# A two-layer decoder step on one core: layers unrolled, projections cut into parts of half the tokens, and the norms laid between the parts

## The chip, the cores and the metric

The kernel runs on one core of a Trainium2 chip. TensorE (PE) multiplies; VectorE (DVE), ScalarE (ACT) and GpSimd (POOL) work on the elements; SyncE (SP) issues most of the transfers. The metric is the device time of one launch, in microseconds (us).

## The reference, cut to what matters

One inference step of two layers, for 512 prompt tokens and 8 sample tokens that share the weights (520 tokens of 1024 features), all in float32:

```python
def decoder_layer(x, mem_kv, past, lp, rel_bias):
    g = lp['norm_g']
    mix, st = mixer_block(rms_norm(x, g[0]), lp, rel_bias, past)
    x = x + rms_norm(mix, g[1])
    x = x + rms_norm(cross_attention(rms_norm(x, g[2]), mem_kv, lp['w_xq'], lp['w_xo']), g[3])
    x = x + rms_norm(swiglu(rms_norm(x, g[4]), lp['w_ffn_in'], lp['w_ffn_out']), g[5])
    return x, st
```

`rms_norm` divides each token by the root of its mean square and multiplies by a gain. `mixer_block` projects the input with `w_in` (queries, keys and values, gates of the attention heads, the inputs of two convolutions, and 3 x 1024 merge gates), runs sparse attention (for the sample tokens over a paged cache), a convolution of 3 taps and one of 31 taps with a LayerNorm behind it, maps each of the three branches to 1024 features, merges them by the sigmoid of the gates, and projects with `w_o`. Cross-attention has 4 heads and 256 memory tokens; the feed-forward part has 2816 hidden features.

## The kernel before, in words

Activations lie transposed in SBUF: 128 features by 520 tokens is a chunk, 8 chunks are one token row of 1024 features (KC = 8). A projection goes in **units** of 128 output features, 512 KB of weights each. Float32 is split in a high and a low part, and a product is three matmuls (low weights by high activations, high by low, high by high) for each chunk and each half of the tokens (HALF = 260), so a unit of 8 chunks is 48 matmuls, issued by `products` (L422). SP loads a unit into a ring of four raw slots (L372); ACT makes the high part (`split_hi`, L381), DVE the low part (`split_lo`, L386), one unit ahead of PE. The matmuls of a layer in these stages: mix 960 in 20 units and 48 more for the head gates (L720), mg (merge gates) 1152, out (the three branch projections, L1753) 384, wo 384, xkv (keys and values of the memory, 256 columns) 192, xq 192, xo 192, fi (feed-forward in) 2112, fo (feed-forward out) 1056: 6672.

The layers run in a hardware loop, and so do groups of four units. Each step of a layer is a block of its own, and a block begins when every engine has ended the one before: the norm in front of mix, mix, convolutions and gathering of new rows (the conv block, L738 to L891), prompt attention, decode (sample attention over the cache), mg, the LayerNorm, out, wo, one block for norms 1 and 2, xkv, xq, cross-attention, xo, one block for norms 3 and 4, fi, fo, norm 5. `norm_block` has ACT square the chunks (L485), PE sum them over the features with 80 small matmuls in the trace (L499), DVE form the mean (L522), POOL raise it to -1/2 (L512), DVE build a diagonal (L526), PE spread it over the partitions (L505), DVE multiply (`t`, L536), and then either ACT and DVE or POOL make the high and low parts (L489, L470) or DVE and POOL add to x (L473). `stage_block` (L1592) converts a source that isn't normed, all 8 chunks of it, before PE starts (L1601 on ACT, L1612 on DVE). Three times in a layer a phase ends: a barrier, and POOL clears each semaphore of it (L143 to L148). The program starts with loads, 40 matmul rows for key biases (L315, two passes each in the trace), transposes of x and of the memory (L329), flips for the bias table (L337) and, in each layer, a block that loads and transposes the small vectors (L614 to L655).

These lines hold the order of the norm's work and the wait at the head of a stage:

```python
                            for c in range(KC):
                                e.wait_ge(sq_ready, KC * k + c + 1)
...
                            e.wait_ge(rstd_ready, k + 1)
...
                        if source is not None:
                            e.wait_ge(op_lo, base + chunks)
                        pe(e)
```

Of the kernel before, what the change touches and what calls it, by code (L numbers as in the profile page):

```python
# [1 line left out]

# [12 lines left out]
F32 = mybir.dt.float32  # L15
F32R = mybir.dt.float32r
I32 = mybir.dt.int32
# [34 lines left out]

V_GAIN, V_MEM, V_CA, V_CB, V_CG, V_CS, V_B1, V_B2, V_CC, V_PE, V_END = 0, 48, 56, 62, 64, 66, 68, 70, 72, 134, 166
RMS_EPS, LN_EPS = 1e-6, 1e-5
SEL_FORCE = 1e6


U_MIX, U_MG, U_OUT, U_WO, U_XKV, U_XQ, U_XO, U_FI, U_FO, U_END = 0, 20, 44, 52, 60, 68, 72, 80, 124, 148
# [64 lines left out]

def build(nc, A, O):
# [9 lines left out]

    @contextmanager
    def phase_semaphores():

        first = len(sems)
        with ExitStack() as scope:
            owner.append(scope)  # L140
            yield
            owner.pop()
            with nc.Block() as block:  # L143
# [7 lines left out]
    def sb(scope, name, shape, dt=F32):  # L151
        return scope.enter_context(nc.sbuf_tensor(name, shape, dt))

    def await_reg(e, s, value):

        e.wait_ge(s, value)
        e.sem_inc(passed, 1)

    with stack:

        xT = sb(stack, "xT", [P, KC, TOK])
        act_hi = sb(stack, "act_hi", [P, KC, TOK], F32R)
        act_lo = sb(stack, "act_lo", [P, KC, TOK], F32R)
        w_raw = sb(stack, "w_raw", [P, RING, KC * P])
        w_hi = sb(stack, "w_hi", [P, 2, KC * P], F32R)
        w_lo = sb(stack, "w_lo", [P, 2, KC * P], F32R)
        ident = sb(stack, "ident", [P, P])
        ones = sb(stack, "ones", [P, P])
        ov = sb(stack, "ov", [P, 2, SELB + 1])
        rt = sb(stack, "rt", [SELB + 1, 2 * P])  # L170
        key_bias = sb(stack, "key_bias", [P, 40, N_HEADS])
        new_bias = sb(stack, "new_bias", [NB, NB, N_HEADS])
        gather_rows = sb(stack, "gather_rows", [P, NB * 8], U32)
        vecs = sb(stack, "vecs", [P, V_END])
        minus_half = sb(stack, "minus_half", [P, NB])
        pg = stack.enter_context(nc.psum_tensor("pg", [P, 2, 2, 512], F32))
        pn = stack.enter_context(nc.psum_tensor("pn", [P, 2, 512], F32))
        pa = [stack.enter_context(nc.psum_tensor(f"pa{i}", [P, 512], F32)) for i in range(2)]
        line_dram = nc.dram_tensor("line_scratch", [N_HEADS, LINE], F32)
# [3 lines left out]
        passed = sem("passed")  # L183
        dve_chain, act_chain, pool_chain = Chain(sem("dve_done")), Chain(sem("act_done")), Chain(sem("pool_done"))
        raw_full = [sem(f"raw_full{i}") for i in range(RING)]
        whi_ready, w_ready = sem("whi_ready"), sem("w_ready")
        unit_done = sem("unit_done")
        evac = [sem("evac0"), sem("evac1")]
        sq_ready, sq_used, ms_ready, rstd_ready = (sem(n) for n in ("sq_ready", "sq_used", "ms_ready", "rstd_ready"))
        diag_ready, rstd_bc, t_ready, hi_ready, even_ended, odd_ended = (sem(n) for n in (  # L190
            "diag_ready", "rstd_bc", "t_ready", "hi_ready", "even_ended", "odd_ended"))
# [6 lines left out]


        with phase_semaphores(), ExitStack() as scope:  # L200
            x_nat = sb(scope, "x_nat", [P, 5, D_MODEL])
            m_nat = sb(scope, "m_nat", [P, 2, D_MODEL])
            m_sq = sb(scope, "m_sq", [P, D_MODEL])
            m_ms = sb(scope, "m_ms", [P, 2])
            m_rstd = sb(scope, "m_rstd", [P, 2])
            memT = sb(scope, "memT", [P, KC, N_MEM])
# [1930 lines left out]
```

## Time and profile before

| what | value |
|---|---|
| time, median of 3 runs (lowest, highest) | 4017.01 us (4013.03, 4021.43) |
| span of the profiled execution | 4001.0 us |
| TensorE busy | 3353.9 us, 84% of the span |
| VectorE, ScalarE, GpSimd busy | 1486.5, 958.4, 348.6 us |
| moved by transfers | 346.88 MB, mean 87 GB/s |

The span is the profiled execution from its first to its last instruction. The profile gives no other time for that execution; the median of the runs is 16.0 us over the span (4017.01 less 4001.0). Busy times are sums over an engine's instructions. A granted clock (PEclk) of 1.0 is 2.4 GHz, 0.5 is 1.2 GHz. A window view gives for a stretch, from a start to an end in us, the length, each engine's busy time with the count of its instructions, the mean granted clock, the busy share of the transfer engines and GB/s.

### The profile page before, as it was taken

How to read it: one execution, taken by the hardware profiler on the slowest of the kernel's cores; microseconds unless marked ns; L12 is line 12 of the kernel's file. 1: busy time of each engine (PE TensorE's matmuls, PEld its weight loads, DVE VectorE, ACT ScalarE, POOL GpSimd, SP SyncE). 2: the span in 40 equal slices, each digit the busy share in tenths (PEclk: the TensorE clock that was granted, in tenths of full speed). 3: DMA queues.
4: the chain of work that ended last, by engine and by line, in shares of the span. 5: the costliest groups of instructions: out<-in, count | busy, mean ns of one | idle time of the engine just before them, and what ended most of it. 6: DMA issues, size and time to landing. Idle time of an engine off the chain costs nothing. (4 is left out here: it accounts for less than half of the span.)

```text
span 4001.0 us, 61151 instructions
## 1 busy us (share of the span) xinstructions
PE 3353.9 (84%) x22906; PEld 3143.2 (79%) x22906; DVE 1486.5 (37%) x3364; ACT 958.4 (24%) x1827; POOL 348.6 (9%) x470
## 2 busy tenths in 40 slices
PE   3878799898988677899939788989979777879997
PEld 2876588887978577899939566888879676879997
DVE  1235533333553322333222454343436523133322
ACT  0223322211222212222212233121212222122221
POOL 1000032221000101000010002222200010010000
PEclk8887788887988676999959779888869878679998
DMA  4220154441322301232223104443313214013321
GB/s 127 64 97 17 56 178 151 137 137 63 95 66 66 140 18 32 80 93 86 67 41 89 72 14 151 148 159 128 132 46 91 58 38 152 17 47 89 94 87 45
DMA packets 353360, 346.88 MB, mean 87 GB/s; under 512 B 36001, under 2 KB 323110, under 8 KB 336238
## 3 DMA queue, kind: packets, MB, share of 16 engines
q1 hardware_dynamic: 334238, 210.34, 17.9%
q0 software_dynamic: 18944, 134.24, 9.7%
q8 instruction: 103, 1.69, 0.2%
q14 instruction: 75, 0.61, 0.1%
HBM read 333.85 MB, written 19.55 MB: 88 GB/s over the span
## 5 line engine op out<-in xcount | busy, mean ns | idle before, releaser
L422 PE MATMUL pg<-act_hi,w_lo 128*128 128x260 f32 x3328 | 682.4, 287 | 115.0 <-PEq L143 42.0
L422 PE MATMUL pg<-act_lo,w_hi 128*128 128x260 f32 x3328 | 679.3, 286 | 0.0
L422 PE MATMUL pg<-act_hi,w_hi 128*128 128x260 f32 x3328 | 679.1, 286 | 0.0
L386 DVE TENSOR_TENSOR w_lo<-w_raw,w_hi 128x1024 fp32r<-128x1024 f32 x296 | 362.5, 1225 | 690.7 <-ACT w_hi L381 682.8
L422 PEld LDWEIGHTS pg<-act_hi,w_lo 128*128 128x128 f32 x3328 | 523.8, 192 | 119.9 <-issue 89.3
L422 PEld LDWEIGHTS pg<-act_hi,w_hi 128*128 128x128 f32 x3328 | 522.3, 192 | 0.0
L422 PEld LDWEIGHTS pg<-act_lo,w_hi 128*128 128x128 f32 x3328 | 522.3, 192 | 0.0
L381 ACT CAST w_hi<-w_raw 128x1024 fp32r<-128x1024 f32 x292 | 305.7, 1047 | 291.3 <-PE pg L422 137.0
L499 PE MATMUL pa<-ones,sq 128*128 128x1 f32 (+1 forms) x960 | 173.4, 305 | 52.9 <-ACT sq L485 52.9
L499 PEld LDWEIGHTS pa<-ones,sq 128*128 128x128 f32 (+1 forms) x960 | 168.6, 263 | 61.1 <-ACT sq L485 57.4
L1418 ACT COPY w_raw<-pg 128x512 f32<-128x512 f32 x144 | 84.4, 586 | 443.1 <-PE pn L1315 421.2
L1391 PE MATMUL pn<-pr,v_sel 128*128 128x8 f32 x1024 | 185.5, 325 | 0.0
L1391 PEld LDWEIGHTS pn<-pr,v_sel 128*128 128x128 f32 x1024 | 184.4, 285 | 0.0
L1291 PE MATMUL pg<-ident,apart 128*128 128x128 f32 x1024 | 161.6, 309 | 14.1 <-DVE apart L1467 14.1
L512 POOL TENSOR_TENSOR r<-ms,minus_half 128x8 f32<-128x8 f32 x12 | 19.7, 1642 | 1647.2 <-DVE ms L523 1647.2
L1291 PEld LDWEIGHTS pg<-ident,apart 128*128 128x128 f32 x1024 | 133.8, 163 | 18.4 <-issue 15.1
L422 PE MATMUL pg<-hid_hi,w_lo 128*128 128x260 f32 x704 | 142.1, 283 | 6.1 <-PEq L1592 6.1
L422 PE MATMUL pg<-hid_hi,w_hi 128*128 128x260 f32 x704 | 141.5, 282 | 0.0
L422 PE MATMUL pg<-hid_lo,w_hi 128*128 128x260 f32 x704 | 141.3, 282 | 0.0
L1315 PEld LDWEIGHTS pn<-q_blk,w_raw 128*128 128x128 f32 x1024 | 134.5, 192 | 6.7
L1244 POOL COPY cell<-gather_rows 128x1 uint32 (+1 forms) x128 | 28.7, 224 | 1268.5 <-POOLq L143 703.7
L1246 POOL DMA_INDIRECT cache<-in_cache_kv,cell x128 | 129.1, 1009 | 70.4 <-POOL cell L1244 70.4
(395 smaller groups left out, 5107.3 us busy)
## 6 DMA issues: line engine op xcount, KB each, us to landing
w_raw<-in_w_ffn_in SPq DMA_DIRECT2D x88, 512.0 KB, 3.8
w_raw<-in_w_in SPq DMA_DIRECT2D x80, 512.0 KB, 3.8
cmem<-in_cache_mem SPq DMA_DIRECT2D x16, 1024.0 KB, 12.9
w_raw<-in_w_ffn_out SPq DMA_DIRECT2D x32, 512.0 KB, 3.7
win<-in_cache_win SPq DMA_DIRECT2D x16, 512.0 KB, 3.6
w_raw<-in_w_o SPq DMA_DIRECT2D x16, 512.0 KB, 3.8
w_raw<-in_w_xkv SPq DMA_DIRECT2D x16, 512.0 KB, 3.8
out_win_sample<-in_cache_win SPq DMA_DIRECT2D x2, 4088.0 KB
```

Source lines behind the costliest of these rows:

```text
L381: e.copy(w_hi[:, slot % 2, :], w_raw[:, slot, :]).then_inc(whi_ready, 1)
L386: e.tensor_tensor(w_lo[:, slot % 2, :], w_raw[:, slot, :], w_hi[:, slot % 2, :].bitcast(F32), ALU.subtract).then_inc(w_ready, 1)
L422: mm = e.matmul(pg[:, tslot, h, 0:wd], w[:, slot % 2, wk], x[:, k0 + k, at:at + wd], start=first and k == 0 and n == 0, stop=last and k == ...
L499: mm = e.matmul(pa[i][0:w, tt:tt + 1], sq[:, c % 2, tt * P:tt * P + w], ones[:, 0:1], start=c == 0 and tt == 0, stop=c == KC - 1, skip_gro ...
L512: e.tensor_tensor(r[:], ms[:], minus_half[:], ALU.pow).then_inc(rstd_ready, 1)
L1244: e.tensor_copy(cell[:, k % 4:k % 4 + 1], gather_rows[:, bass.ds(b * TILES + k, 1)]).then_inc(cell_set, 1)
L1246: e.indirect_dma_start(out=cache[:, k % 4, :], out_offset=None, in_=rows_dram, in_offset=bass.IndirectOffsetOnAxis(ap=cell[:, k % 4:k % 4 ...
L1291: mm = e.transpose(pg[:, 0, kv, at:at + P], apart[:, k % 2, 2 * kv + g, 2 * pair:2 * pair + 2, :].rearrange("p t d -> p (t d)"), ident[:])
L1315: mm = e.matmul(pn[:, 0, (4 * k + t) * 8:(4 * k + t + 1) * 8], k_sel[:, t * P:(t + 1) * P], q_of(b), start=True, stop=True)
L1391: e.matmul(pn[:, 1, 8:16], v_sel[:, par, t, :], pr[:, t, :], start=t == 0, stop=False)
L1418: e.copy(k_sel[:], pg[:, 1, 0, :]).then_inc(ks_ready, 1)
```

## The change

The two layers are written out in Python, so no loop is left around the projections. A stage is a list of `Part`s (unit, tile, half of the tokens, a range of chunks), and the lists decide the order of PE's matmuls: `head` does half 0 of four tiles first, in two runs of four chunks, then half 1; `both` does one tile's halves in turn; `tail` ends with all of half 0 before all of half 1. Each (tile, half) has one of four banks of PSUM. Raw weights have three slots, split weights four, and splits run two units ahead.

The norms are no blocks now. An `Edge` joins one stage to the next: when a part is done ACT squares it and copies it (`post_evict`), POOL adds the squares (`post_sum`), PE sums them over the features in three matmuls (`stats`), POOL raises to -1/2 (`power`), PE spreads (`spread`), DVE multiplies (`t_step`), DVE for even and POOL for odd chunks adds to x (`x_step`), ACT makes the high part and the squares for the next norm (`hi_step`), DVE the low part (`lo_step`), POOL adds the squares (`acc_step`). The 1/rms of the norm ahead of a product isn't applied to the activations any more; DVE multiplies the product by it when it empties PSUM (`scaled_evict`). PE waits per chunk (`gate`), not for a whole conversion. Of the other steps: setup work lies between the units of the first mix, the head gates are tile 20 of mix, the LayerNorm's pieces lie between mg's last tiles, the 31-tap convolution is done in 4 taps per mg unit instead of 3, the memory's conversion lies under wo, the memory cache is loaded at the start of cross-attention (it was ahead of it, L1812), sums of the merge are on POOL, and the key biases are made in layer 0's conv block from two loads into one buffer, the second of which waits for the matmuls of the first. Semaphores are cleared after setup, and in each layer after decode and after cross-attention. The bodies of prompt attention, decode and cross-attention are as they were.

The core of the diff:
```diff
-            def norm_block(norms):
...
-                            for c in range(KC):
-                                e.wait_ge(sq_ready, KC * k + c + 1)
-                                for tt in range(5):
-                                    w = P if tt < 4 else NB
-                                    mm = e.matmul(pa[i][0:w, tt:tt + 1], sq[:, c % 2, tt * P:tt * P + w], ones[:, 0:1],
-                                                  start=c == 0 and tt == 0, stop=c == KC - 1, skip_group_check=True)
...
-                        if source is not None:
-                            e.wait_ge(op_lo, base + chunks)
-                        pe(e)
...
+def head(tiles, cuts0=((0, 4), (4, 4)), cuts1=((0, 4), (4, 4))):
+
+    return [Part(t, t, h, k, kn, k, k == 0, k + kn == KC) for h, cuts in enumerate((cuts0, cuts1)) for k, kn in cuts for t in tiles]
+def both(tiles):
+    return [Part(t, t, h, 0, KC, 0, True, True) for t in tiles for h in range(2)]
+def tail(tiles):
+    return [Part(t, t, h, 0, KC, 0, True, True) for h in range(2) for t in tiles]
...
+        mix = lambda: Stage(self, 21, head(range(4)) + both(range(4, 21)))
...
+            self.wo.append(Stage(self, 8, head(range(4), ((0, 7), (7, 1)), ((0, KC),)) + tail(range(4, 8))))
+            self.xkv.append(Stage(self, 8, [Part(t, t, 0, 0, KC, 0, True, True) for t in range(8)]))
+            self.xq.append(Stage(self, 4, head(range(4))))
+            self.xo.append(Stage(self, 4, [Part(t // 2, t, h, XH * (t % 2), XH, 0, True, True) for h in range(2) for t in range(KC)]))
+            self.fi.append(Stage(self, 44, head(range(4)) + both(range(4, 44))))
...
+                for k in range(x.kn):
+                    if gate is not None:
+                        signal, count = gate(x.half, x.xk + k)
+                        e.wait_ge(signal, count)
...
+        def post_evict(e, ed, i, t, h):
+            st, n = ed.before, 2 * KC * ed.post + i
+            tile_done(e, st, t, h, handed=True)
...
+            e.activation(ed.sqa[:, i % 3, :], bank_of(st, t, h), ACT.Square).then_inc(sqa_ready, 1)
+            e.copy(ed.Y[:, h, t, :], bank_of(st, t, h)).then_inc(emptied(st, t, h), 1)
+        def post_sum(e, ed, i, t, h):
...
+                e.tensor_tensor(ed.acc1[:, h, :], ed.acc1[:, h, :], ed.sqa[:, i % 3, :], ALU.add).then_inc(acc1_ready, 1)
+        def stats(e, ed, i):
...
+            for s, a in enumerate((0, P, HALF - P)):
+                mm = e.matmul(pa[0][:, 3 * i + s:3 * i + s + 1], acc[:, h, a:a + P], ones[:, 0:1], start=True, stop=True)
...
+        def hi_step(e, ed, h, c):
...
+            e.activation(act_hi[:, h, c, :], x, ACT.Copy, scale=col(ed.gain_pre + c)).then_inc(hi_ready, 1)
...
+            e.activation(ed.sqb[:, (KC * h + c) % 3, :], x, ACT.Square).then_inc(sqb_ready, 1)
+        def scaled_evict(e, ed, st, t, h, dst, handed=False):
+            tile_done(e, st, t, h, handed)
+            e.wait_ge(rbc_ready, 2 * ed.pre + h + 1)
+            e.tensor_tensor(dst, bank_of(st, t, h), rbc[:, h, :], ALU.mult).then_inc(emptied(st, t, h), 1)
...
+                        if L == 0:
+                            for i in range(2):
+                                if i:
+                                    e.wait_ge(keys_mm, 1)
+                                e.dma_start(keys[:], C["keys"].ap()[:, i * 20 * P:(i + 1) * 20 * P]).then_inc(keys_in, 16)
+                        e.wait_ge(nt_used, 11)
...
+                    run(e, wo, act, 0, 17, w_gate)
+                    stats(e, ed, 0)
+                    run(e, wo, act, 17, 18)
+                    spread(e, ed, 0)
+                    run(e, wo, act, 18, 20)
+                    run(e, skv, mem_act, 0, 1, m_gate, N_MEM)
+                    stats(e, ed, 1)
```

PE's program at its start. Names: `x_nat` is x as loaded, `keys` and `rel` make the key biases, `sq` are squares of a norm, `act_hi` and `w_lo` a high and a low part. Before:

```order
L313 MATMUL pn<-line1h,rel 8x512 x2
L315 MATMUL pg<-rel,keys 128x8 x40
L329 MATMUL pa<-ident,x_nat 128x128 x32
L329 MATMUL pa<-ident,x_nat 128x8 x8
L329 MATMUL pa<-ident,m_nat 128x128 x16
L337 MATMUL pg<-toep_up,flip 128x512 x8
...
L650 MATMUL pa<-ident,rows_pe 128x32
...
L505 MATMUL pn<-diag,ones 128x260 x2
L476 UNCONDITIONAL_BRANCH
L712 UNCONDITIONAL_BRANCH
L422 MATMUL pg<-act_hi,w_lo 128x260 x2
```

And now:

```order
L989 MATMUL pn<-ident,rows_g 128x112
L997 MATMUL pa<-ident,x_nat 128x128 x16
L997 MATMUL pa<-ident,x_nat 128x8 x4
...
L1001 MATMUL pn<-ident,rows_m 128x96
L1002 MATMUL pn<-ident,rows_c 128x124
L563 MATMUL pg<-act_hi,w_lo 128x260
```

The first product stands behind the transposes of x and of small vectors alone; the key biases (now L1193, 40 rows in layer 0's conv block), the memory and the bias table come later, and there are no sums of squares ahead of it.

PE's program between wo and xkv in layer 0. `mem_hi` is the high part of the memory, `acc_wo` the sum of squares, `r_t` the 1/rms per token. Before:

```order
L422 MATMUL pg<-act_hi,w_hi 128x260 x2
...
L1592 UNCONDITIONAL_BRANCH
L491 UNCONDITIONAL_BRANCH
L499 MATMUL pa<-ones,sq 128x1 x4
L499 MATMUL pa<-ones,sq 8x1
...
L505 MATMUL pn<-diag,ones 128x260 x2
...
L422 MATMUL pg<-mem_hi,w_lo 128x256
```

And now, around the third `stats` and `spread`, which lie inside xkv:

```order
L563 MATMUL pg<-mem_hi,w_hi 128x256
...
L636 MATMUL pa<-ident,r_t 128x128 x2
L636 MATMUL pa<-ident,r_t 128x4
L563 MATMUL pg<-mem_hi,w_lo 128x256
```

Two norms of 40 small rows each stood between the last product of wo and the first of xkv; now three rows of `stats` and two of `spread` stand between products, four times from wo's tail to xq.

POOL's program at the norms between xo and fi. `t_xo` is the scaled product, `sqa_xo` and `sqb_xo` squares for the norm behind xo and the one ahead of fi. Before:

```order
L512 TENSOR_TENSOR r<-ms,minus_half 128x8
L473 TENSOR_TENSOR xT<-xT,t 128x520 x4
...
L470 TENSOR_TENSOR act_lo<-t,act_hi 128x520 x4
...
L148 ISA x17
```

And now, from the norm's first power to the second:

```order
L607 TENSOR_TENSOR acc_xo<-acc_xo,sqa_xo 128x260 x2
L628 TENSOR_TENSOR r_t<-ms_t,minus_half 128x3
...
L656 TENSOR_TENSOR xT<-xT,t_xo 128x260
L607 TENSOR_TENSOR acc_xo<-acc_xo,sqa_xo 128x260
L675 COPY acc_xo<-sqb_xo 128x260
...
L678 TENSOR_TENSOR acc_xo<-acc_xo,sqb_xo 128x260
```

POOL had 10 instructions of a norm pair here and clears of semaphores behind them; it now has 44 of half the width (16 sums behind xo, 16 ahead of fi, 8 additions to x, 4 powers), and PE's `stats` waits for its sums.

## Rows read from the trace of the kernel before

**Rows 1.** Page, busy time of each engine and its instructions; granted clock in 40 slices.

```profile
span 4001.0 us, 61151 instructions
...
PE 3353.9 (84%) x22906; PEld 3143.2 (79%) x22906; DVE 1486.5 (37%) x3364; ACT 958.4 (24%) x1827; POOL 348.6 (9%) x470
...
PEclk8887788887988676999959779888869878679998
```

**Rows 2.** Windows, layer 0: start:end length, busy by engine, clock, DMA share, GB/s.

```profile
0.00:134.90 134.90, 55.60 (x242) 44.82 (x242) 29.53 (x56) 15.55 (x23) 17.79 (x28) 0.73 0.37 96
134.90:264.90 130.00, 125.73 (x1009) 125.35 (x1009) 25.94 (x22) 31.64 (x42) 0.00 (x0) 0.96 0.27 73
264.90:293.50 28.60, 10.86 (x77) 8.83 (x77) 17.56 (x45) 9.44 (x24) 0.00 (x0) 0.67 0.56 215
1008.40:1013.60 5.20, 0.05 (x1) 0.08 (x1) 0.00 (x0) 0.00 (x0) 0.00 (x0) 0.50 0.00 2
1013.60:1179.30 165.70, 147.10 (x1184) 145.30 (x1184) 98.87 (x168) 46.10 (x61) 1.68 (x1) 0.93 0.33 89
1179.30:1237.30 58.00, 47.78 (x384) 47.57 (x384) 42.18 (x65) 12.62 (x16) 0.00 (x0) 0.91 0.25 73
1237.30:1285.10 47.80, 47.75 (x384) 47.62 (x384) 9.18 (x8) 10.78 (x14) 0.00 (x0) 0.97 0.27 77
1285.10:1353.10 68.00, 33.94 (x169) 31.27 (x169) 24.64 (x50) 19.16 (x34) 15.14 (x10) 0.52 0.07 23
1353.10:1410.70 57.60, 51.20 (x384) 50.30 (x384) 14.43 (x12) 15.28 (x22) 0.00 (x0) 0.91 0.65 229
1411.60:1521.00 109.40, 90.06 (x471) 85.41 (x471) 25.67 (x41) 14.89 (x45) 0.00 (x0) 0.65 0.03 10
1525.80:1867.20 341.40, 315.08 (x2472) 311.48 (x2472) 127.16 (x149) 95.43 (x126) 15.12 (x10) 0.91 0.26 76
...
1611.00:1867.20 256.20, 256.18 (x2112) 255.97 (x2112) 98.55 (x108) 68.71 (x87) 0.00 (x0) 0.99 0.31 90
1870.20:1997.20 127.00, 126.96 (x1056) 126.75 (x1056) 28.18 (x23) 27.04 (x30) 0.00 (x0) 1.00 0.26 76
1997.20:2097.10 99.90, 33.72 (x172) 30.68 (x172) 21.09 (x37) 17.55 (x27) 15.41 (x11) 0.52 0.19 35
3953.00:4001.00 48.00, 23.56 (x125) 19.79 (x124) 16.42 (x27) 5.57 (x9) 8.31 (x5) 0.61 0.11 45
```

**Rows 3.** Groups by line on DVE and ACT: count, busy us, mean ns, idle before.

```profile
L386 DVE TENSOR_TENSOR w_lo<-w_raw,w_hi 128x1024 fp32r<-128x1024 f32 x296 | 362.5, 1225 | 690.7 <-ACT w_hi L381 682.8
...
L1669 DVE SCALAR_TENSOR_TENSOR y_c<-u_c,vecs,y_c 128x512 f32<-128x512 f32 x120 | 90.0, 750 | 2.8
...
L1669 DVE SCALAR_TENSOR_TENSOR y_c<-us_c,vecs,y_c 128x8 f32<-128x8 f32 x120 | 27.2, 227 | 4.2
...
L2030 DVE SCALAR_TENSOR_TENSOR silu<-thf,pg 128x520 f32<-128x520 f32 x44 | 30.6, 696 | 115.8 <-ACT thf L2021 115.8
...
L381 ACT CAST w_hi<-w_raw 128x1024 fp32r<-128x1024 f32 x292 | 305.7, 1047 | 291.3 <-PE pg L422 137.0
```

**Rows 4.** Groups by line on POOL, and the key-bias matmuls on PE.

```profile
L473 POOL TENSOR_TENSOR xT<-xT,t 128x520 f32<-128x520 f32 x24 | 40.1, 1672 | 43.8 <-DVE t L536 43.8
...
L470 POOL TENSOR_TENSOR act_lo<-t,act_hi 128x520 fp32r<-128x520 f32 x24 | 30.8, 1284 | 59.5 <-ACT act_hi L489 59.5
...
L512 POOL TENSOR_TENSOR r<-ms,minus_half 128x8 f32<-128x8 f32 x12 | 19.7, 1642 | 1647.2 <-DVE ms L523 1647.2
...
L315 PE MATMUL pg<-rel,keys 32*128 32x8 f32 x80 | 17.2, 356 | 0.0
```

**Rows 5.** Timeline, SP's queue: start, us, line, transfer.

```profile
274.10 11.48 SPq L754 DMA_DIRECT2D out_kv_sample<-nat  x1
...
1376.08 8.04 SPq L1812 DMA_DIRECT2D cmem<-in_cache_mem  x8
```

**Rows 6.** Timeline, PE at the start of fi.

```profile
1611.53 0.64 PE L422 MATMUL pg<-act_lo,w_hi 128*128 128x260 f32 x2
```

More of the change, by code:

```diff
@@ L121, in restart, with __init__, take @@
         self.n = 0
+class Strip:
+    def __init__(self, nc, start, end):
+        self.nc, self.at, self.end = nc, -(-start // 32) * 32, end
+    def take(self, name, shape, dt=F32):
+        size = -(-4 * int(np.prod(shape[1:])) // 32) * 32
+        start, self.at = self.at, self.at + size
+        assert self.at <= self.end, (name, self.at, self.end)
+        return self.nc.alloc_sbuf_tensor_at(name, shape, dt, offset=start)
+@dataclass
+class Part:
+    unit: int
+    tile: int
+    half: int
+    wk: int
+    kn: int
+    xk: int
+    first: bool
+    last: bool
+    to: str = "pg"
+    end: int = 0
+    bank: int = 0
+    turn: int = 0
@@ L124, in build, with order, step @@
+@dataclass
+class Edge:
+    post: int
+    pre: int
+    seq: int
+    before: Stage
+    gain_post: int
+    gain_pre: int
+    Y: object = None
+    acc1: object = None
+    acc2: object = None
+    sqa: object = None
+    sqb: object = None
+    t: object = None
+    free: tuple = (0, 0)
+    @property
+    def order(self):
+        return [(x.tile, x.half) for x in self.before.parts if x.last]
+    def step(self, i):
+        return self.seq + (i if self.post >= 0 else i - 2) + 1
 def build(nc, A, O):
@@ new lines, in _, with flips @@
+                    run(e, mix0, act, at(10), at(15))
+                    def flips(i):
+                        e.wait_ge(toep_in, 16 * (i + 1))
+                        e.wait_ge(line_ready, 1)
+                        for n in range(i * HPG, (i + 1) * HPG):
+                            if n >= 2:
+                                e.wait_ge(flip_used, n - 1)
+                            e.matmul(pn[:, n % 2, :], flip[:], toep_up[:, n % HPG, :], start=True, stop=True).then_inc(flip_done, 1)
+                    flips(0)
@@ new lines, in build @@
+        for_dec.at = ends_at
+        for_dec.end = ends_at + 2048 + 384
+        second = for_dec.take("second", [P, 2, 2 * P + 1])
+        for_dec = Strip(nc, late_at, z_at)
+        gate_dg = for_dec.take("gate_dg", [NG_W, NB, NG_W])
+        gate_bc = for_dec.take("gate_bc", [P, NB, NG_W])
+        for_dec = Strip(nc, decode_at, limit)
+        xkv0 = for_dec.take("xkv0", [P, 2, 512])
+        xkv = (xkv0, xkv1)
+        k_sel = for_dec.take("k_sel", [P, 512])
+        cv = for_dec.take("cvs", [P, 2, P])
@@ L790, in _ @@
                         mm.then_inc(pem, 1)
+                        if L == 0:
+                            for i in range(2):
+                                e.wait_ge(keys_in, 16 * (i + 1))
+                                for b in range(20):
+                                    at = (20 * i + b) * N_HEADS
+                                    mm = e.matmul(pg[:, 1, 1, at:at + N_HEADS], keys[:, b * P:(b + 1) * P], rel[:], start=True, stop=True)
+                                mm.then_inc(keys_mm, 1)
                         e.wait_ge(ua_ready, 1)
@@ L2079, in build @@
+        rows_out = Strip(nc, mid_at, limit).take("rows_out", [P, 5, D_MODEL])
+        with phase_semaphores("end"):
             y_tr, y_cp, y_out = sem("y_tr"), sem("y_cp"), sem("y_out")
```

2448 lines of the change are left out of this document (1483 added, 965 removed).

## The prediction

> **What bounds the kernel now.** I read the page first, then windows by stage, then groups by line. PE is busy 3353.9 us of 4001.0, far above every other engine [rows 1], so the question is where PE stands still and where it runs at the lower clock. The row of the clock gives both places: full in some slices, half in others. The windows sort them. In fi 2112 matmuls fill 256.2 us without a hole, in fo 1056 fill 127.0 us [rows 2]: 127.0/1056 = 120.3 ns a matmul, so a unit of 48 takes 5.77 us. This part can't get faster unless the number of matmuls falls, and it doesn't. DVE and ACT need 1.225 and 1.047 us a unit to split the weights [rows 3]; SP's transfers use about a third of the time.
>
> The other kind of window is the norm. Between wo and xkv 68.0 us pass, with PE busy 33.94 at clock 0.52; between the end of fo and the next mix 99.9 us, PE busy 33.72 at 0.52; before the first product of all 134.9 us [rows 2]. PE's busy time there is mostly small matmuls at half speed, and one engine after another has the word. So each stage has its own limit: projections are PE's, seams are a chain over five engines.
>
> **The change, part by part.** Times are of the profiled execution (span 4001.0); its sum is made against the span, and 16.0 us are added at the end, since the median of the runs stands so much higher.
>
> *Start of layer 0.* From 0 to the conv block it takes 134.9 + 130.0 = 264.9 us [rows 2]. Now x is the first large load. 2.1 MB at the 229 GB/s seen around xq is 9 us, say 10 with the issue; about half (an estimate) of PE's 21 us of transposes and flips is x's (55.60 less 17.2 for the keys [rows 4] and about 17 for a norm, half of 33.94), so transposes end near 18.5, and the first product begins about 22.5 after one high and one low part. Four head tiles need 23.1 us and wait some 5 for chunks: 51. Seventeen units more are 98.1, the other half of the transposes and flips, laid between them, 11, and 3 for its waits: 163; 5 for the last eviction and the block. The conv block starts at 168: **-97**. Ends: -75 if weights and x share the queue so that the first product comes at 45; -110 if nothing waits.
>
> *Keys in the conv block.* The trace shows this block's queue stuck: one small output transfer cost SP 11.48 us of issuing, until 285.58 [rows 5], because the copy of the sample window, issued earlier in the block, fills the queues. SP is free of it 20.7 us into the block; I take 24 until a load issued behind the copy has landed, and the first half of the keys is such a load. On the path now: 24 + 8.6 (half of 17.2 [rows 4]) + 2.5 for the second load (an estimate; it waits for PE, and the outputs wait behind it on SP) + 8.6 + 5 for the ends, then the 3 us lead of prompt attention: 51.8 against 28.6 [rows 2]: **+23**. Ends: +8 if the load gets through half-way in the copy; +30 if the second load is as slow as the copy. DVE's 17.56 us in this block lie under it.
>
> *Each layer.* One clearing of semaphores less ahead of decode, a longer one behind it (5.20 us with PE idle now [rows 2]) and the first split behind that: +2.6. mg and LayerNorm, 165.7 us: 1152 matmuls are 138.6; 2 for the clock's climb; about 6 for LayerNorm's own sums and spreading between tiles; and DVE has 1.225 + 0.70 (eviction, as L2030) + 4 x (0.750 + 0.227) = 5.83 us a unit [rows 3], about 6.1 with the gaps between dependent instructions, against PE's 5.77, over 16 units 5 us, of which banks hide some: 3. Together 149.6, **-16**. Out, 58.0: the conversion that stood ahead of wo goes, 384 x 0.1203 = 46.2, **-12**. Wo, 47.8: 49.2 with the first chunks' wait, +1.4. From wo's end to xq's end 68.0 + 57.6 = 125.6: two norms run under xkv's 192 matmuls; 46.2 remain for xkv and xq, and I allow 9.5 for five small-matmul stops and for xq's first chunk, 55.7, **-70**. Cross to xo +2: the memory cache now is loaded at cross's start. Its issue took 8.04 us [rows 5], the window in which it was moved had 229 GB/s, so its 8.4 MB take 37 us at most at that rate, shared then with weights; transfers are idle in cross-attention (share 0.03 of 109.4 us [rows 2]), and the sample part, which needs it, comes behind the prompt part, some 40 us in (an estimate: over a third of the stage). Hidden, with little to spare; without that cover 37 us a layer. Xo to fi's end, 341.4: 2304 matmuls are 277.2, 3 for two climbs, and 16 for the head of fi (power 1.642 on POOL [rows 4], spreading, then t, x, high, low for the first chunk, and splits that stand behind xo's units): 296, **-45**. Fo -1.5. A layer: 2.6 - 16 - 12 + 1.4 - 70 + 2 - 45 - 1.5 = -138.5; two layers **-277**.
>
> *Between the layers.* From fo's end to the first product 99.9 us [rows 2], and 24.7 for the first four units. Now 23.1 + 8 for the chain until the first low part + 7.5 for the second half's chunks, small stops and the climb = 38.6, **-86**. Ends of the seam terms: nothing below, if the chains overlap in full; above, half of now's 68.0 for each, as a rival below. The rest of mix (130.0 for 1008 matmuls in layer 0, 8.7 over 121.3) loses another -6.
>
> *End.* 48.0 us from fo's end [rows 2]: half 0 of the last norm runs under the last tile's half 1, the chain of half 1 and the transposes stay, 25: **-23**.
>
> Sum: -97 + 23 - 277 - 92 - 23 = -466. Each place where PE stops long enough to come back at 1.2 GHz costs about 2 us: at fi's start two matmuls end in 0.64 us [rows 6], and 256.2 is 2.1 over 2112 x 0.1203. I allow seven more of these, 14. 4001.0 - 466 + 14 = 3549, and 16 on top: **3565 us**.
>
> *The unknown price is POOL's.* An edge with two norms has 16 + 16 sums, 8 additions and 4 powers. The trace has no 128x260 sum on POOL. From below half of 1.284 us, 0.64; from above the whole 1.672 [rows 4]. I take 0.84, half of the nearest row, an addition of two SBUF operands. Then an edge is 40 x 0.84 + 4 x 1.642 = 40 us of POOL, spread over two tails and a head of about 60 us. At 0.64 the waits shrink; at 1.67 it is 73 us and POOL sets the seam.
> The rows show POOL's addition (1.672) slower than its subtraction of the same size (1.284); beside the first DVE runs its own addition of x and t, beside the second mostly a product that reads PSUM. The Trainium skill, "SBUF — State Buffer", section "Who interferes with whom", says why this may be and speaks against the change: a DVE instruction with two SBUF inputs and a GpSimd instruction that reads SBUF shut each other out for a whole instruction. By that rule a sum that meets a weight split waits up to 1.225 us more, 0.64 + 1.225 = 1.87, and an edge's 12 sums and additions between the first spread and the next stage's first statistics could take 12 us longer. The 0.39 us in the rows agree in sign, and nothing in this trace shows it against a split.
>
> **Rivals.**
> *Seams stay, shorter (POOL).* For: `stats` waits for POOL's last sum, and POOL's program is in a fixed order, so an addition to x stands behind sums. Against: POOL is busy 9% now. With 1.67 instead of 0.84, 12 instructions between spread and statistics cost 10 us a half; one half of it shown at five seams, and splits late behind it, with half clock in each: 50 to 130 us. **About 3650**.
> *Nearly no stalls.* The allowances above (9.5, 16, 3 and 6 a layer, 14 for the clock, 8 between layers, 23 for keys) halve: -65. **About 3500**.
> *The change doesn't do what it says.* Post-norms of the last tile can't overlap; if each seam also waits for the whole other half (splits, banks still full), five seams give back 34 us each, half of 68.0: **about 3735**.
> *Slower than before.* PE's program is straight, without loops. If PE were fed more slowly, each of 13,344 projection matmuls would lengthen. The 452 us forecast are gone at 34 ns each, a spacing of 154 ns instead of 120. Place: fi and fo, where nothing else can wait. For: idle time put down to PE's own sequencer at block starts. Against: the loops' bodies already hold 192 matmuls, and the spacing in them is that of the engine, not of its feed. **About 4060** at 157 ns. The Trainium skill, "Runtime: NRT & Kernel Launch", section "Instruction fetch mechanics", has instructions prefetched in sequence and only taken branches stall; no run here shows straight code of this length.
>
> **How the numbers follow.** Forecast 0.50, with a range of its own of 3525 to 3610: keys (-15, +7), start (-13, +22), conv-tap and head allowances. POOL seams 0.24, stall-free 0.13, not as described 0.08, slower 0.04; 0.01 for no change. Slower and unchanged are 0.05 together. The range of 8 in 10 takes in the forecast, stall-free from 3490, and POOL seams to 3680. A change of 0.2% is about what can be told from none here.
>
> **What would show it.** Right: the first matmul of L563 near 22 us and the conv block near 168; key biases some 24 us into that block; 120 ns in fi and fo; no stretch with clock near 0.5 but attention; holes of under 8 us between wo and xq and ahead of fi; mg near 150. Wrong: POOL sums of 1.5 us or more with PE waiting for them; PE waiting for splits in mg by more than 0.5 us a unit; cross-attention waiting for the memory cache; PE spacing above 125 ns; holes of 20 us at seams.

## The result, and the profile after

The changed kernel takes 3592.40 us (median of 4 runs, 3591.09 to 3594.55), against 4015.02 for the kernel before (4 runs, three of them those of the table under "Time and profile before"): a ratio of 0.8967, 95% interval 0.8943 to 0.8990. The forecast was 3565, with 3490 to 3680 for 8 in 10. The profiled execution has a span of 3590.3 us and took 3592.02.

The page of the changed kernel, the lines that answer to [rows 1]:

```profile
span 3590.3 us, 57484 instructions
...
PE 3210.2 (89%) x22207; PEld 3012.9 (84%) x22207; DVE 1573.9 (44%) x3626; ACT 950.6 (26%) x2036; POOL 524.5 (15%) x706
...
PEclk9957898887799966999999678888879999599999
```

TensorE has 144 us less to do, nearly all of it small matmuls of norms that ran at half clock; its idle time fell from 647 us (4001.0 less 3353.9) to 380. VectorE and GpSimd do more than before. The sums of squares on TensorE, in the page of the kernel before:

```profile
L499 PE MATMUL pa<-ones,sq 128*128 128x1 f32 (+1 forms) x960 | 173.4, 305 | 52.9 <-ACT sq L485 52.9
```

In the changed kernel they are 144 matmuls (L619) of 19.0 us together.

Windows of the changed kernel, columns as in [rows 2]. In layer 0: first product to conv block, conv block, mg, out, wo, xkv with xq, fo; then the conv block of layer 1 and the end. Below them, two longer stretches, fo's start to the end of the next mix, and fo's start in layer 1 to the end of the program; then xo with fi, fo's end to the end of mix, and cross-attention in layers 0 and 1.

```profile
25.10:172.70 147.60, 137.46 (x1066) 131.10 (x1067) 57.39 (x84) 31.61 (x50) 13.11 (x15) 0.97 0.46 124
172.70:226.70 54.00, 34.79 (x156) 31.38 (x156) 18.17 (x47) 9.99 (x24) 0.00 (x0) 0.50 0.34 130
946.70:1093.80 147.10, 146.92 (x1196) 146.48 (x1197) 111.28 (x184) 44.48 (x59) 2.27 (x1) 0.98 0.34 90
1093.80:1152.00 58.20, 49.22 (x386) 47.95 (x385) 27.43 (x44) 11.04 (x14) 20.46 (x14) 0.97 0.26 73
1152.00:1206.40 54.40, 50.08 (x400) 49.29 (x399) 20.17 (x28) 24.96 (x54) 15.97 (x21) 0.97 0.35 107
1206.40:1264.40 58.00, 51.63 (x420) 50.66 (x419) 34.25 (x57) 23.18 (x50) 24.54 (x27) 0.97 0.33 92
...
1686.70:1814.60 127.90, 127.90 (x1068) 127.72 (x1066) 32.28 (x34) 33.45 (x57) 12.15 (x17) 1.00 0.36 95
...
1956.30:1984.90 28.60, 16.76 (x76) 13.64 (x76) 17.56 (x45) 9.79 (x24) 0.00 (x0) 0.51 0.56 218
3565.60:3590.30 24.70, 9.50 (x52) 7.15 (x52) 16.12 (x31) 0.65 (x2) 6.83 (x9) 0.69 0.23 87
...
1686.50:1954.10 267.60, 260.60 (x2114) 258.95 (x2112) 86.69 (x116) 65.66 (x111) 35.87 (x45) 0.97 0.34 88
3437.50:3590.30 152.80, 137.59 (x1122) 135.04 (x1120) 45.95 (x63) 31.05 (x56) 18.94 (x26) 0.95 0.25 77
1386.80:1686.70 299.90, 290.02 (x2354) 288.71 (x2355) 155.98 (x235) 99.96 (x185) 35.86 (x44) 0.97 0.30 87
1814.60:1954.10 139.50, 132.50 (x1045) 131.04 (x1044) 54.41 (x83) 32.20 (x54) 23.72 (x29) 0.94 0.31 81
...
1264.40:1386.80 122.40, 97.05 (x472) 92.10 (x472) 28.37 (x47) 17.67 (x51) 0.00 (x0) 0.61 0.20 78
3021.90:3137.50 115.60, 89.98 (x472) 85.34 (x472) 28.41 (x47) 17.70 (x51) 0.00 (x0) 0.65 0.21 82
```

The seams are where the time came from: wo's end to xq's end is 58.0 us (125.6 before), xo's start to fi's end 299.9 (341.4), fo's end to the end of the next mix 139.5, the end 24.7 (48.0) [rows 2]. Two windows stand out on the other side. Out takes 58.2 us for 384 matmuls, no better than before with the wait ahead of wo in it, and layer 0's conv block 54.0 where layer 1's takes 28.6.

What TensorE waited for in all, in the view of waits (total us, times, longest):

```profile
PE pg L563 <- DVE w_lo L540: 31.5, 10, 8.7
...
PE pn L563 <- DVE G L2108: 16.4, 12, 1.9
...
PE pg L1193 <- DMA keys<-c_keys: 13.4, 2, 9.3
...
PE pn L636 <- POOL r_t L628: 7.4, 5, 2.5
```

The longest entry, for low parts of weights, lies for 16.7 us at mg's start behind decode (8.7 and 8.0 in the two layers); the others are waits of up to 3.1 us where a stage starts. The waits for GpSimd's powers (L628) are small. The one for `G` (L2108) comes twelve times, up to 1.9 us each, and TensorE's product into `pn` that waits stands in out alone.

### The profile page after: what moved, and what is told of

Its sections match the earlier page's. It is cut to its first block and busy times, and to the rows that moved or that the text cites. A ratio compares the mean times of both kernels' runs of the same rounds, so it can differ in the third digit from the quotient of the medians.

```text
span 3590.3 us, 57484 instructions
## 1 busy us (share of the span) xinstructions
PE 3210.2 (89%) x22207; PEld 3012.9 (84%) x22207; DVE 1573.9 (44%) x3626; ACT 950.6 (26%) x2036; POOL 524.5 (15%) x706
## 5 line engine op out<-in xcount | busy, mean ns | idle before, releaser
L563 PE MATMUL pg<-act_hi,w_lo 128*128 128x260 f32 x3360 | 972.0, 289 | 72.5 <-DVE w_lo L540 31.5
L563 PE MATMUL pg<-act_hi,w_hi 128*128 128x260 f32 x3360 | 962.9, 287 | 0.0
L563 PE MATMUL pg<-act_lo,w_hi 128*128 128x260 f32 x3360 | 961.1, 286 | 0.0
L563 PEld LDWEIGHTS pg<-act_lo,w_hi 128*128 128x128 f32 x3360 | 647.1, 193 | 0.5 <-issue 0.5
L563 PEld LDWEIGHTS pg<-act_hi,w_hi 128*128 128x128 f32 x3360 | 646.9, 193 | 0.0
L540 DVE TENSOR_TENSOR w_lo<-w_raw,w_hi 128x1024 fp32r<-128x1024 f32 (+1 forms) x290 | 354.3, 1226 | 475.4 <-ACT w_hi L534 473.1
L534 ACT CAST w_hi<-w_raw 128x1024 fp32r<-128x1024 f32 (+1 forms) x290 | 296.8, 1033 | 298.2 <-PE pg L563 118.2
L1665 PE MATMUL pg<-xkv,w 128*128 128x256 f32 x1024 | 262.4, 402 | 0.5
L1665 PEld LDWEIGHTS pg<-xkv,w 128*128 128x128 f32 x1024 | 198.7, 205 | 27.2 <-ACT second L1763 0.7
L1673 PEld LDWEIGHTS pn<-q_blk,k_sel 128*128 128x128 f32 x1024 | 134.5, 192 | 6.7
```

The lines of the kernel that those rows point to most:

```text
L534: e.copy(w_hi[:, v % RING, 0:n], w_raw[:, v % RAW, 0:n]).then_inc(whi_ready, 1)
L540: e.tensor_tensor(w_lo[:, v % RING, 0:n], w_raw[:, v % RAW, 0:n], w_hi[:, v % RING, 0:n].bitcast(F32), ALU.subtract).then_inc(w_ready, 1)
L563: mm = e.matmul(out, w[:, v % RING, wk], a[x.half][:, x.xk + k, :], start=x.first and k == 0 and n == 0, stop=x.last and k == x.kn - 1 and ...
L1665: e.matmul(pg[:, 1, 1, kv * 256:(kv + 1) * 256], w1[:, kv, 2 * (k % 4) + pair, :], xkv[k % 2][:, kv, pair * 256:(pair + 1) * 256], start=k ...
L1673: mm = e.matmul(pn[:, 0, (4 * k + t) * 8:(4 * k + t + 1) * 8], k_sel[:, t * P:(t + 1) * P], q_of(b), start=True, stop=True)
```

## The experiments

Times scatter by as much as most of the effects sought (below), so each experiment is judged by the windows of the stage that it changes; its whole time is given beside that.

**A circle in out.** The timeline of the changed kernel in out, one tile of the merge, all engines (TensorE's other products left out):

```profile
1109.54 1.70 POOL L1958 TENSOR_TENSOR G<-G 128x520 f32<-128x520 f32 x1 [4.83 <-DVE G L2108]
...
1111.31 1.30 POOL L1960 TENSOR_TENSOR G<-G 128x520 f32<-128x520 f32 x1
1112.64 0.64 ACT L2017 ACTIVATE act_hi<-G 128x520 fp32r<-128x520 f32 x1 [6.33 <-POOL G L1960]
1113.19 1.04 ACT L534 CAST w_hi<-w_raw 128x1024 fp32r<-128x1024 f32 x1
1114.26 1.23 DVE L540 TENSOR_TENSOR w_lo<-w_raw,w_hi 128x1024 fp32r<-128x1024 f32 x1 [4.19 <-ACT w_hi L534]
1115.40 0.69 DVE L2105 SCALAR_TENSOR_TENSOR G<-G,pg 128x520 f32<-128x520 f32 x1
...
1117.42 0.39 PE L563 MATMUL pn<-src_hi,w_lo 128*128 128x260 f32 x1 [1.88 <-DVE G L2108]
1117.44 1.69 POOL L1958 TENSOR_TENSOR G<-G 128x520 f32<-128x520 f32 x1 [4.83 <-DVE G L2108]
```

From one merge sum to the next 7.90 us pass (1117.44 less 1109.54), and no engine is busy all that time. ScalarE's program has the high part of a tile, which waits for GpSimd's sums, ahead of the split of the weights that VectorE must split before it can merge the next tile. So each tile's merge waits for the sums of the last. The first edit opens the circle by order alone:

```diff
+                    def high_of(m):
+                        e.wait_ge(sum_odd, 2 * (KC * L + m + 1))
+                        e.activation(act_hi[:, :, m, :], halves(G[:, m, :]), ACT.Copy, scale=0.5).then_inc(mrg_hi, 1)
                     for m in range(KC):
                         ahead_hi(e, out.u0 + m, wo.u0 + 2)
-                        e.wait_ge(sum_odd, 2 * (KC * L + m + 1))
-                        e.activation(act_hi[:, :, m, :], halves(G[:, m, :]), ACT.Copy, scale=0.5).then_inc(mrg_hi, 1)
+                        if m:
+                            high_of(m - 1)
+                    high_of(KC - 1)
```

> In the out stage ScalarE makes the high part of a merged tile one tile later, behind the weight split that it stood ahead of; nothing else changes. Theory: the stage runs in a circle over engines, merge on VectorE 2.0 us, two sums on GpSimd 3.0, high part 0.64, ScalarE's split 1.04, VectorE's split 1.23, which is the 7.9 us a tile that the trace shows, against 5.77 of products; with the high part behind the split the circle is open, out falls from 58.2 us to 47 to 49 in each layer, and the time by 18 to 22 us, to about 3572. Rival: GpSimd's sums are slow because VectorE holds the SBUF port, and the merge waits for them anyway; then out stays over 55 us and the time falls by less than 6 us.

Window of out in layer 0:

```profile
1100.90:1147.20 46.30, 46.30 (x388) 46.30 (x387) 35.23 (x45) 12.01 (x15) 26.30 (x14) 1.00 0.33 92
```

58.2 us became 46.3 in layer 0 and 46.2 in layer 1, with TensorE busy throughout; 3574.60 us (3563.91 to 3578.83). GpSimd needs longer for its sums now (26.30 us busy against 20.46): the second sum of a tile and the next weight split on VectorE meet, and six times in this window the sum takes 2.17 us for 1.30 and the split 2.33 for 1.23. That costs nothing here. The rival is out. The second way to shorten the circle undoes a part of the change, with ScalarE's order left:

```diff
                 @block.gpsimd
...
-                        e.tensor_tensor(g[0], g[0], g[1], ALU.add).then_inc(sum_odd, 1)
...
                 @block.vector
...
                         mm.then_inc(merged, 1)
+                        e.wait_ge(merged, KC * L + m + 1)
+                        e.tensor_tensor(g[0], g[0], g[1], ALU.add).then_inc(sum_odd, 1)
```

The second sum moves with the first.

> The two sums of the merge in out go back from GpSimd to VectorE (0.70 us each, as before the change); order on ScalarE as in the changed kernel. Theory of the circle: 2.0 + 1.4 + 0.64 + 1.04 + 1.23 = 6.3 us a tile, so out takes about 51 us in each layer, 13 to 15 us less in all, about 3578. Rival (the sums aren't in any circle, VectorE is what out lacks): VectorE gets 11 us more work a layer, and out stays at 58 us or grows.

```profile
1088.10:1136.70 48.60, 47.64 (x387) 46.55 (x386) 37.29 (x59) 12.63 (x16) 0.00 (x0) 1.00 0.31 88
```

48.6 us in each layer, somewhat better than the 51 worked out; 3574.18 us (3562.26 to 3578.91). VectorE has 10 us more work and the stage is still 9.6 shorter. Both agree: what out lacked was no engine; it was held by the length of the chain through three of them, VectorE, GpSimd and ScalarE.

**Keys in layer 0's conv block.** The first edit moves only the copy that the prediction held responsible:

```diff
-                        e.dma_start(o_layer("win_sample")[:, :, 0:WINDOW - 1].rearrange("o b w k g d -> (o b) w (k g d)"),
-                                    A["cache_win"][L:L + 1][:, :, 1:WINDOW].rearrange("o b w k g d -> (o b) w (k g d)")).then_inc(outs, 16)
...
+                        e.dma_start(O["win_sample"][L:L + 1][:, :, 0:WINDOW - 1].rearrange("o b w k g d -> (o b) w (k g d)"),
+                                    A["cache_win"][L:L + 1][:, :, 1:WINDOW].rearrange("o b w k g d -> (o b) w (k g d)")).then_inc(win_out, 16)
                         e.wait_ge(mn_cp, 4)
```

> The 4 MB copy of the sample window is issued behind the loads of the memory cache in cross-attention, not at the start of the conv block, in both layers. Theory: the copy is what the key-bias loads wait for; layer 0's conv block falls from 54.0 us to about 36, layer 1's from 28.6 to about 25, and nothing comes back in cross-attention, whose transfers are idle: 18 to 24 us less, about 3571. Rival: the two dependent loads and the 80 small matmuls set the block by themselves, or cross-attention waits for the memory cache beside the copy: the block stays over 48 us or cross grows by 10, and the time falls by less than 6 us.

PE's timeline in the conv block of the changed kernel, the two runs of key-bias matmuls:

```profile
198.57 8.70 PE L1193 MATMUL pg<-rel,keys 32*128 32x8 f32 x40 [9.33 <-DMA keys<-c_keys]
211.34 8.70 PE L1193 MATMUL pg<-rel,keys 32*128 32x8 f32 x40 [4.08 <-DMA keys<-c_keys]
```

The same view with the copy moved:

```profile
188.63 8.70 PE L1191 MATMUL pg<-rel,keys 32*128 32x8 f32 x40
201.26 8.70 PE L1191 MATMUL pg<-rel,keys 32*128 32x8 f32 x40 [3.94 <-DMA keys<-c_keys]
```

And windows of both conv blocks and of cross-attention in layer 0:

```profile
172.20:216.50 44.30, 34.69 (x156) 31.33 (x156) 18.19 (x47) 9.97 (x24) 0.00 (x0) 0.50 0.20 64
1944.50:1972.70 28.20, 16.82 (x77) 13.67 (x77) 17.55 (x45) 9.77 (x24) 0.00 (x0) 0.51 0.23 77
1252.80:1375.20 122.40, 96.94 (x473) 92.08 (x472) 28.44 (x47) 17.74 (x51) 0.00 (x0) 0.61 0.28 112
```

The wait of 9.33 us ahead of the first half is gone, so the copy did hold it; cross-attention is as long as without it, 122.4. But the block falls by 9.7 only, to 44.3: neither the theory's 36 nor the rival's 48. A block of 36 us would have needed the keys' matmuls some 8 us into it (25.9, where they began, less 18); at half clock TensorE's other small matmuls take until 16.4 (188.63 less 172.20). Layer 1's block hardly changes (28.2 us, for the 25 expected). The time is 3581.45 us (3575.47 to 3586.81). The next edit removes both waits: all keys are loaded in setup, on three groups of partitions:

```diff
-        keys = for_conv.take("keys", [NBUCK, 20 * P])
+        keys = Strip(nc, decode_at, limit).take("keys", [3 * NBUCK, 14 * P])
...
-                                    mm = e.matmul(pg[:, 1, 1, at:at + N_HEADS], keys[:, b * P:(b + 1) * P], rel[:], start=True, stop=True)
+                                mm = e.matmul(pg[:, 1, 1, b * N_HEADS:(b + 1) * N_HEADS], keys_of(b), rel_of(b), start=True, stop=True)
```

> All keys of the bias are loaded during setup into free space (on three groups of partitions, with three copies of the bias table); their 40 matmul rows stay where they are in layer 0's conv block. Theory: the block's 54.0 us are 28.6 of before, 9.3 of wait for the first load (behind the window copy), 4.1 for the second, and the rest of 17.4 us of matmuls at half clock; without the two waits it is 40 to 41 us. Rival: the block is held by something else that takes the same time, its outputs behind the copy of the window on SP's queue; then it stays over 48 us.

Windows of the conv block and of all between the first product and it:

```profile
176.10:211.50 35.40, 29.67 (x157) 26.83 (x157) 18.17 (x47) 9.86 (x24) 0.00 (x0) 0.60 0.46 180
24.20:176.10 151.90, 138.16 (x1067) 131.80 (x1067) 57.34 (x84) 31.59 (x50) 13.07 (x15) 0.96 0.46 125
```

And the keys' row in PE's timeline, without a wait:

```profile
187.78 17.48 PE L1195 MATMUL pg<-rel,keys 32*128 32x8 f32 x80
```

The block is 35.4, better than 40 to 41: both waits are gone, and in this execution the clock rose inside the block (0.60 against 0.50). The early loads cost mix 4 us (151.9 against 147.6; TensorE's second wait for a weight split there is 6.10 us, 2.49 in the changed kernel). 3585.75 us (3577.57 to 3589.53). The third place for them is mix itself:

```diff
+                    for b in range(40):
...
+                        mm = e.matmul(pa[1][:, b * N_HEADS:(b + 1) * N_HEADS], keys_of(b), rel_of(b), start=True, stop=True)
...
                     run(e, mix0, act, at(17), at(19))
```

> The keys are loaded as in e5, and their matmul rows stand in layer 0's mix between tiles 16 and 17; also ScalarE's order in out as in e1. Theory: conv block 28 to 29 us in layer 0 as in layer 1 (25 less), mix longer by what 40 small rows take beside full-size products (9 to 18 us), out 46.2 in both layers (24 less): 33 to 40 us less than the changed kernel, 3552 to 3560. Rival: weights, splits or evictions stand still behind the small rows and mix loses 25 us or more, so that moving the keys gives nothing and the time is that of e1, about 3570.

```profile
192.90:220.80 27.90, 11.91 (x76) 9.54 (x76) 17.55 (x45) 9.86 (x24) 0.00 (x0) 0.62 0.56 218
24.40:192.90 168.50, 155.98 (x1147) 149.25 (x1147) 58.02 (x86) 31.53 (x50) 13.17 (x15) 0.92 0.42 112
```

The keys' matmuls in mix:

```profile
143.50 14.77 PE L1061 MATMUL pa<-rel,keys 32*128 32x8 f32 x80
```

The conv block gives 26.1 us back, mix takes 20.9 of them, more than the 9 to 18 expected: the keys' matmuls take 14.77 us beside full products, not much less than the 17.4 alone, the wait for the second weight split is 2.2 longer (4.72 against 2.49), and the other 4 weren't followed. In time it is 3560.43 us (3559.14 to 3567.65), most of it from out. The keys belong in the conv block, where TensorE has room, with their loads ahead.

**Waiting by chunk.**

```diff
-            return lambda h, c: (lo_ready, 2 * KC * ed.pre + KC * h + c + 1)
+            return lambda h, c: (lo_ready, 2 * KC * ed.pre + KC * h + 4 * (c // 4) + 4)
```

> Behind the norms, TensorE waits for chunks in fours instead of one by one (the first product of a head waits for low part 4 instead of 1). Theory: the gain at the seams comes from laying norms beside other parts, and waiting by chunk gives little, since the runs of four chunks over four tiles last 11.5 us and the next chunks come in less: 1 to 3 us at each of the four heads that wait, 4 to 10 us in all, 3597 to 3603. Rival: waiting by chunk is what hides the conversions; then each head of xq, fi and mix pays the three chunks that it now waits for, 4 us with a restart at half clock, at six heads and in both halves: 20 us or more.

Windows of xo with fi, and of fo's end to mix's end:

```profile
1385.50:1686.50 301.00, 286.99 (x2354) 286.51 (x2355) 155.89 (x235) 99.95 (x185) 35.86 (x44) 0.98 0.30 87
1814.40:1954.80 140.40, 128.80 (x1045) 128.44 (x1044) 54.41 (x83) 32.19 (x54) 23.71 (x29) 0.95 0.32 81
```

1.1 and 0.9 us longer than in the changed kernel (299.9 and 139.5). TensorE starts fi 5 us later, and its waits at fi's head are 4 us longer in all: 7.0, 0.4 and 4.9 us in place of five of 0.8 to 2.7. But its busy time in the stretch is 3.0 us less (286.99 against 290.02), at a mean clock of 0.98 against 0.97, which takes most of that back. The theory holds, at its lower end; the time (3603.36 us, 3598.43 to 3605.55) is longer by more than these stages explain, and the rest lies in stages that the edit doesn't touch: in the profiled execution layer 1's cross-attention alone is 7 us longer (122.6 against 115.6).

**GpSimd's part in the seams.**

```diff
-            if c % 2 == 0:
-                x_step(e, ed, h, c)
+            x_step(e, ed, h, c, True)
```

(and GpSimd's own calls do nothing)

> All additions to x are on VectorE (0.45 us each); GpSimd, which had the odd chunks (0.75 to 0.92 us each, in a fixed order between its sums), keeps the sums and powers. Theory: the heads of xq, fi and mix are held by VectorE's chain and by the weight splits in it, and by the climb of the clock; GpSimd isn't the limit, so from xo's start to fi's end stays within 3 us of 299.9, mix of layer 1 within 3 us of 139.5 with its lead. Rival: GpSimd's place in the chain (its order, and the port that it shares with VectorE) sets the seams; then each of these stretches falls by 5 us or more, and the time by 15 or more.

```profile
1385.90:1685.60 299.70, 289.15 (x2354) 287.60 (x2355) 161.57 (x243) 100.28 (x185) 29.11 (x36) 0.97 0.30 87
1813.60:1954.00 140.40, 131.89 (x1045) 130.37 (x1044) 58.06 (x90) 32.62 (x54) 16.39 (x21) 0.94 0.32 81
```

299.7 and 140.4: within 1 us, though GpSimd is relieved of 7 us in each. Its additions aren't the bound of the seams. Its sums and powers stayed where they were; in the changed kernel TensorE's waits for them add up to 14.6 us over both layers. 3589.60 us (3584.20 to 3606.19).

**One half beside the other.**

```diff
-            + [part(KC - 1, i, h) for h in range(2) for i in range(3)])
+            + [part(KC - 1, i, h) for i in range(3) for h in range(2)])
```

> Fo's last tile is computed with its two halves in turn, so the first half of the tokens ends 2 us before the second and not 8; TensorE's statistics of both halves stand behind the last product. Nothing else changes. Theory: a norm of one half hides beside the products of the other; without that the chain of the first half lies bare after fo, 5 to 7 us more between fo and mix in layer 0 and 4 to 7 more behind fo in layer 1: 9 to 14 in all. Rival: the seam is held by the second half's chain or by VectorE and the splits, whatever the first half does: both stretches stay within 2 us.

Windows of fo's start to mix's end, and of fo's start in layer 1 to the end (267.6 and 152.8 in the changed kernel):

```profile
1682.00:1953.10 271.10, 260.88 (x2114) 259.24 (x2112) 86.97 (x116) 65.60 (x111) 37.10 (x45) 0.96 0.33 87
3439.80:3596.90 157.10, 139.40 (x1121) 136.72 (x1120) 46.14 (x63) 31.06 (x56) 19.07 (x26) 0.93 0.25 75
```

3.5 and 4.3 us longer, 7.8 in all. Behind fo it is 4.8 and 5.6, 10.4 in all, as the theory has it (9 to 14); fo itself is 1.3 us shorter in each layer, without the statistics in its last tile. 3599.81 us (3597.93 to 3605.05). Laying one half's norm beside the other half's products is worth some 4 us net at a seam of this shape.

**Both repairs.** ScalarE's order of e1, and the keys of e5 with their loads later in setup:

> The order on ScalarE of e1 and the keys of e5, their loads later in setup (behind the weights of tile 14), so that mix doesn't wait for them. Theory: the two waits are independent and add: out 46 us in both layers (24 less), layer 0's conv block about 35 (18 less), mix of layer 0 as in the changed kernel: 40 to 44 us less than the changed kernel in these stages, 3548 to 3556 with the scatter of decode and cross-attention. Rival: what is gained in out is lost in wo, or the later loads still hold weights or the bias table up: less than 32 us.

```profile
170.90:211.30 40.40, 34.91 (x157) 31.49 (x157) 18.18 (x47) 10.01 (x24) 0.00 (x0) 0.50 0.41 158
1086.90:1133.20 46.30, 46.30 (x388) 46.30 (x387) 35.22 (x45) 12.01 (x15) 26.34 (x14) 1.00 0.32 92
```

Out gives 11.9 us (12.0 in layer 1), the conv block 13.6 (at clock 0.50, so not the 18 of e5), and mix of layer 0 is no longer than in the changed kernel (146.1 against 147.6): some 39 in these stages, just under the 40 to 44 expected. The time is 3558.18 us (3553.69 to 3561.32), 2 above the expected range and 34 under the changed kernel's median, and no run of one reaches those of the other; its ratio to the kernel before is 0.8874 (0.8862 to 0.8886).

## Why the prediction was right, and where it was off

The direction and the mechanism were right: projections kept their price (fo 127.9 us for 1056 matmuls, 121 ns each), and the seams gave the time. Of the 410.7 us between the two spans 143.7 are TensorE's busy time and 267.0 its idle time. Which part of the change gave how much at the seams is argued and not shown: the experiments on single parts (e3, e7, e9) move 0 to 6 us a seam, and no run takes the rest apart. Term by term, with what was measured:

- *Start*, 168: 172.7. *Keys*, 51.8 for the block: 54.0, made as described but for sizes: the first half came at 25.9 us for 24, the second load cost 4.1 for 2.5.
- *mg*, 149.6: 147.1. *Wo's end to xq's end*, 55.7: 58.0. *Xo to fi's end*, 296: 299.9. *Fo*, 125.5: 127.9. *Fo's end to the end of mix*, with the lead of the conv block, 138: 141.7 (1814.6 to 1956.3). *End*, 25: 24.7. *Cross-attention* waits nowhere for the memory cache, as forecast. These are within 5 us each, but for cross-attention, which came out at 122.4 and 115.6 for 117 (more on it in the last section).
- *Wo*, 49.2: 54.4. TensorE does 18 products and then waits 3.2 us for the seventh low part of the merge; some 16 products behind it start 0.22 us apart instead of 0.12, at half clock, and the statistics lie in wo's tail. Only a wait of 3.0 was in the sum. E1 takes 1.1 of it back.
- *Out* is the step that failed, as mis-sized work: "384 x 0.1203 = 46.2" took TensorE for the bound, with no term for the sums that had moved to GpSimd and the conversion that had moved into ScalarE's loop. They closed a circle of 7.9 us a tile. 12 us a layer, 24 in all; e1 and e4 show it.
- *16 us on top of the span* was wrong. Every execution with both on record takes 1.7 or 1.8 us over its span (3592.02 for 3590.3). By that the profiled execution of the kernel before took about 4003 us, a quick one among executions of 3992.46 to 4023.61. The sum for the span, 3549, was 41 us under the 3590.3 measured, and the 16 hid part of this: that 3565 came within 28 us is in part luck.
- *14 us for the clock* aren't to be seen as a term of their own; the terms that exceed their forecast by 2 to 5 us hold such restarts, as wo's does.
- *The stall-free rival*: the allowances that it halves add up to 114 us by its own list, so half is 57 and not 65, and its time about 3508. That changes no reading.
- One sign didn't come: the conv blocks of both layers, and not attention alone, ran at a clock near 0.5 (0.50 and 0.51).

The price of GpSimd's sum was taken well: 0.75 to 0.91 us in the mean (0.84 taken). Additions to x took longer, 0.85 to 1.07 by edge, and powers less, 0.91 for the 1.642 taken.

Groups by line on GpSimd in the changed kernel, its slowest and its quickest kind of sum:

```profile
L678 POOL TENSOR_TENSOR acc_wo<-acc_wo,sqb_wo 128x260 f32<-128x260 f32 x28 | 25.5, 912 | 2.6 <-ACT sqb_wo L668 0.3
...
L607 POOL TENSOR_TENSOR acc_fo<-acc_fo,sqa_fo 128x260 f32<-128x260 f32 x28 | 21.0, 751 | 187.6 <-ACT sqa_fo L597 187.6
```

And the timeline between xo and fi, two sums on GpSimd and a weight split on VectorE:

```profile
1407.31 0.74 POOL L607 TENSOR_TENSOR acc_xo<-acc_xo,sqa_xo 128x260 f32<-128x260 f32 x1
1408.55 1.50 POOL L607 TENSOR_TENSOR acc_xo<-acc_xo,sqa_xo 128x260 f32<-128x260 f32 x1 [0.50 <-ACT sqa_xo L597]
...
1408.22 1.23 DVE L540 TENSOR_TENSOR w_lo<-w_raw,w_hi 128x1024 fp32r<-128x1024 f32 x1 [2.24 <-ACT w_hi L534]
```

A sum that starts 0.33 us into a weight split takes 1.50 us where one without takes 0.74: it ends 0.60 us after the split. So the rule of the Trainium skill, "SBUF — State Buffer", section "Who interferes with whom", agrees with this trace to 0.15 us (0.60 against 0.74): the second of the two is shut out for what is left of the first. It is no single case: of the 216 sums and additions in this trace (L607, L656, L678) 20 start inside a weight split, and each ends 0.59 to 0.62 us after the split. It was right on the meeting and not on the seam: such meetings are few, the sums' mean is 0.75 to 0.91, and e7's stretches are as long with the additions gone from GpSimd.

Of the rivals, that GpSimd keeps the seams long fell by the price of its sums (0.75 to 0.91, where it took 1.67), by TensorE's 14.6 us of waits for its sums and powers and, for its additions, by e7; that there are nearly no stalls, by the two windows of 58.2 and 54.0; that the change doesn't do what it says, by the seams' windows; that straight code is fed too slowly, by 121 ns in fo. Sequential prefetch, as the Trainium skill has it ("Runtime: NRT & Kernel Launch", section "Instruction fetch mechanics"), agrees with that row.

What remains open: the seams' gain wasn't taken apart by cause, as said; 3 to 4 us more than forecast in xo with fi weren't split further; and what sets the clock in cross-attention wasn't tried.

## What to carry to other kernels

Take the norms out from between the products: here that took 68 us a layer between wo and xq, by fewer small matmuls and by norms that run beside products, which weren't measured apart. One half's norm beside the other half's products is worth some 4 us of a seam (e9). When work moves to another engine, follow the chain through all engines once round, from a tile to the next, and compare it with the bound engine's time for a tile, since an engine's next step stands behind the one that waits, as ScalarE's split did in out; a step that waits must not stand ahead of one that the next tile needs. And read an experiment of a few us in the windows of its own stage, not in the whole time.

## What was not expected of the hardware

A stage that TensorE half fills doesn't keep one length, though its instructions are the same. Cross-attention took 122.4 us in layer 0 and 115.6 in layer 1 of one execution, with the same waits but granted clocks of 0.61 and 0.65; layer 0's conv block with early keys took 35.4 us at clock 0.60 in e5 and 40.4 at 0.50 in e8. In the profiles of the changed kernel and the nine experiments, cross-attention from its first matmul to the next product took 121.5 to 123.5 us in 15 of 20 layers and 114.8 to 117.2 in five; in the kernel before it took 114.2 in both. So the forecast's 2 us more for it is 7 in most layers; why the changed kernel lands there more often isn't shown. A stage that keeps TensorE filled repeats: mg took 146.9 to 147.5 us in all ten.

Whole times scatter too. The changed kernel's four executions lie within 3.5 us (3591.09 to 3594.55), those of the kernel before within 29 (3992.46 to 4021.43). But e1 and e7, whose stages are nearly all the same as the changed kernel's, spread over 15 and 22 us, so the four don't show that it repeats better.
